# Expert weights of a mixture-of-experts layer loaded in pairs of chunks

## What is computed

```
logits = xf @ w_router + b_router
top_v, top_i = lax.top_k(logits, 4)              # 4 of 32 experts for each token
def expert_block(xblk, e):
    hmid = xblk @ w_up[e] + b_up[e]              # w_up[e]:   1024 x 2048, 8 MB
    hg = minimum(hmid[:, :1024], 7.0)
    hl = clip(hmid[:, 1024:], -7.0, 7.0)
    act = hg * sigmoid(1.702 * hg) * (hl + 1.0)
    return act @ w_down[e] + b_down[e]           # w_down[e]: 1024 x 1024, 4 MB
```

## Time and profile before

| | |
|---|---|
| three timed runs | 1762.39, 1768.26, 1769.11 us; median 1768.26 |
| profiled execution | 1768.84 us, its span 1767.0 us |
| mean granted clock of PE | 0.891 |
| PE busy | 1400.2 us, 79% of the span |
| DVE, ACT, POOL busy | 30%, 13%, 14% |
| HBM read, written | 463.20 MB, 18.74 MB |
| chain that ended last | PE 32%, issue 20%, DMA 10% of the span |
| experts | from 718 us to the end of the loads at about 1720 us |

### The profile page before, as it was taken

The page is one execution under the profiler, slowest core; times in us unless marked ns, Lnnn a source line. Parts: engine busy times, 40 slices in busy tenths (PEclk is TensorE's granted clock), DMA queues, the critical chain, the costliest instruction groups (busy, mean ns, idle before and its releaser), DMA issues.

```text
span 1767.0 us, 30847 instructions
## 1 busy us (share of the span) xinstructions
PE 1400.2 (79%) x11033; PEld 779.5 (44%) x11034; DVE 529.4 (30%) x1242; ACT 229.3 (13%) x556; POOL 247.9 (14%) x352
## 2 busy tenths in 40 slices
PE   5899999978779797666699989668588598766950
PEld 4677777757778454222233433223133133222320
DVE  2899464463441522411111121111111011100114
ACT  2111232222111101000000000000000000000002
POOL 2008301113311520100000000000000000000002
PEclk9999999989985898788899989899789799888975
DMA  7977565351001175499999779999999799999994
GB/s 150 230 147 131 95 109 133 55 151 65 0 1 38 58 220 194 179 416 419 416 420 418 293 298 419 418 418 419 417 419 417 319 410 417 420 417 419 418 378 143
DMA packets 177331, 481.65 MB, mean 273 GB/s; under 512 B 16187, under 2 KB 104891, under 8 KB 144457
## 3 DMA queue, kind: packets, MB, share of 16 engines
q1 hardware_dynamic: 163579, 459.17, 70.7%
q0 software_dynamic: 3920, 15.27, 2.6%
q10 hardware_dynamic: 9792, 6.70, 1.2%
HBM read 463.20 MB, written 18.74 MB: 273 GB/s over the span
## 4 chain that ended last, share of the span: by engine, by line
PE 32%; issue 20%; DMA 10%; DVE 3%; ACT 2%; SPq 2%; POOL 1%; POOLq 0%; DVEq 0%; ACTq 0%
PE bank L950 11%; DMA arena<-in_w_up 10%; PE bank L962 6%; PE bank L918 3%; PE bank L869 2%; PE bank L857 2%; PE bank L936 2%; PE bank L797 2%; PE bank L841 1%; SPq L376 1%; SPq L379 1%; ACT gate L1209 1%; POOL qkv L559 1%; DVE gate L1654 1%; DVE xrow L1699 1%
## 5 line engine op out<-in xcount | busy, mean ns | idle before, releaser
L950 PE MATMUL bank<-arena,gate 128*32 128x512 f32 x3264 | 411.0, 633 | 145.4 <-DMA arena<-in_w_up 145.3
L950 PEld LDWEIGHTS bank<-arena,gate 128*32 128x32 f32 x3264 | 107.7, 113 | 407.2 <-issue 300.1
L636 PE MATMUL bank<-arena 128*128 128x304 f32 x1024 | 269.1, 426 | 5.8 <-DMA arena<-in_w_in 5.1
L1653 DVE TENSOR_SCALAR gate<-bank 128x256 f32<-128x256 f32 x51 | 21.6, 424 | 835.3 <-PE bank L950 835.3
L636 PEld LDWEIGHTS bank<-arena 128*128 128x128 f32 x1024 | 197.9, 194 | 75.8 <-DMA arena<-in_w_in 5.6
L962 PE MATMUL bank<-arena,gate 128*32 128x256 f32 x3264 | 189.6, 384 | 36.3 <-ACT gate L1209 36.3
L559 POOL TENSOR_TENSOR qkv<-qkv 128x192 f32<-128x192 f32 x52 | 32.8, 631 | 940.1 <-DVE qkv L1627 940.1
L962 PEld LDWEIGHTS bank<-arena,gate 128*32 128x32 f32 x3264 | 122.3, 111 | 91.2 <-issue 49.0
L1320 DVE SCALAR_TENSOR_TENSOR acc<-arena,pcol,acc x240 | 126.5, 603 | 0.1
L918 PE MATMUL bank<-qkv 128*32 128x256 f32 (+1 forms) x1248 | 90.2, 406 | 10.4 <-POOL qkv L563 10.4
L936 PE MATMUL bank<-qkv 128*128 128x512 f32 x102 | 60.0, 671 | 39.6 <-DVE gate L1654 28.2
(11 more groups left out here) (308 smaller groups left out, 1327.9 us busy)
## 6 DMA issues: line engine op xcount, KB each, us to landing
arena<-in_w_up SPq DMA_DIRECT2D x256, 1024.0 KB, 12.4
arena<-in_w_down SPq DMA_DIRECT2D x256, 512.0 KB, 8.8
arena<-in_w_in SPq DMA_DIRECT2D x64, 512.0 KB, 9.9
y_d<-gate ACTq DMA_DIRECT2D x204, 32.0 KB, 5.3
y_d<-zs POOLq DMA_DIRECT2D x1, 4608.0 KB, 17.9
arena<-in_w_conf_out SPq DMA_DIRECT2D x8, 512.0 KB, 5.1
arena<-in_state_dn_S SPq DMA_DIRECT2D x8, 512.0 KB, 7.2
arena<-in_w_dn_out SPq DMA_DIRECT2D x1, 4096.0 KB, 17.0
```

The lines of the kernel that those rows point to most:

```text
L636: last = mm(bank[2 * (j % 2) + f][:, 0:T], wring[:, j, k, P * f:P * (f + 1)], rhs[:, k, :], start=(k == 0), stop=(k == KC - 1))
L950: last = mm(hidden(q)[v], xgT[:, i, SL * q0:SL * (q0 + 1)], parts(wup[k], q)[v], start=False, stop=(k == KC - 1), skip_group_check=True)
```

## The change

Two neighbouring chunks are loaded by one transfer. An expert has four transfers of 2 MB for `w_up` and four of 1 MB for `w_down` in place of eight and eight, and the semaphores `up_in` and `down_in` are four each. SP waits once for each pair, until the second chunk of the pair was used (`used + (k + 1)`). PE still goes chunk by chunk and still waits before each, on the pair's semaphore. The buffers, their sizes and places, the order of the loads and all arithmetic stay.

```diff
+        wup2 = [arena[:, 4096 * ((k + 2) % 4):4096 * ((k + 2) % 4 + 1)].rearrange("p (a n) -> p a n", a=2) for k in range(4)]
+        wdn2 = [arena[:, A_PROJ + 2048 * k:A_PROJ + 2048 * (k + 1)].rearrange("p (a n) -> p a n", a=2) for k in range(4)]
...
-        up_in = [sem(f"up_in{i}") for i in range(KC)]
-        down_in = [sem(f"down_in{i}") for i in range(KC)]
+        up_in = [sem(f"up_in{i}") for i in range(KC // 2)]
+        down_in = [sem(f"down_in{i}") for i in range(KC // 2)]
...
             def load_up(e, k):
-                sp.dma_start(wup[k], w_up_v[:, e, k, :]).then_inc(up_in[k], 16)
+                sp.dma_start(wup2[k // 2], w_up_v[:, e, k:k + 2, :]).then_inc(up_in[k // 2], 16)
...
             def load_down(e, k):
-                sp.dma_start(wdn[k], w_dn_v[:, e, k, :]).then_inc(down_in[k], 16)
+                sp.dma_start(wdn2[k // 2], w_dn_v[:, e, k:k + 2, :]).then_inc(down_in[k // 2], 16)
...
-            for k in range(KC):
+            for k in range(0, KC, 2):
                 load_down(0, k)
...
-            for k in range(4):
+            for k in range(0, 4, 2):
                 load_up(0, k)
             sp.wait_ge(s["o_mm_done"], 6)
-            for k in range(4, KC):
+            for k in range(4, KC, 2):
                 load_up(0, k)
...
-                for k in range(KC):
-                    sp.wait_ge(s["up_used"], used + k)
+                for k in range(0, KC, 2):
+                    sp.wait_ge(s["up_used"], used + (k + 1))
                     load_up(e, k)
-                for k in range(KC):
-                    sp.wait_ge(s["down_used"], used + k)
+                for k in range(0, KC, 2):
+                    sp.wait_ge(s["down_used"], used + (k + 1))
                     load_down(e, k)
...
-                    pe.wait_ge(up_in[k], landed)
+                    pe.wait_ge(up_in[k // 2], landed)
...
-                    pe.wait_ge(down_in[k], landed)
+                    pe.wait_ge(down_in[k // 2], landed)
```

## The result

| | before | after |
|---|---|---|
| median of seven runs each | 1768.26 us (1762.39 to 1771.29) | 1777.02 us (1770.54 to 1781.55) |
| profiled execution, its span | 1768.84, 1767.0 us | 1770.54, 1768.8 us |
| ratio after to before | | 1.0055, 95% interval 1.0038 to 1.0073 |

What follows compares the result with a forecast made beforehand. The DMA rate was taken to bound the expert stretches, and PE the pauses between. Release +3.2, landing +1.9 and fewer transfers -3.0 gave +2.1 us, a forecast median of 1770.5 us, range 1760 to 1781 us.

Steps and rivals of the forecast that it cites:

- rival 1: Before each expert's down loads: refill of `w_down` comes too late, up to 14 us more, 1785 us; chance 0.10.
- the forecast's own bounds: All terms taken at their extremes: from +7.9 us to -10.3 us for the whole kernel.
- What bounds the kernel: Expert part: DMA rate sets the end in stretches at 414 to 416 GB/s; PE sets it at the pauses between.
- Fewer transfers: Expert loads: eight of sixteen transfers go, 0.0125 us each, saving 3.0 us in 30 experts.
- Later release: After pauses and at loop start, an expert's first transfer is issued one chunk later: +3.2 us.
- the joints: Loop start and pauses where DMA engines wait for PE; three count, costing 1.08, 1.06 and 1.07 us.
- Later landing: Where PE takes the lead, a chunk waits until both of its pair have landed: +1.9 us.
- (a): In front of the pause at 978 us: chunks 6 and 7 both follow the later landing, 0.9 us more.
- (b): In front of the pause at 1402 us: two chunks instead of one follow the landing of chunk 3, +0.5 us.
- Rivals 2 and 3: Transfers dearer, saving 13 us, 1760 us, chance 0.07; pair moves at another rate, 1% giving 1780 or 1761 us, chance 0.07.
- What the profile would show: Profile after: merged counts, 414 to 418 GB/s, first issue near 731.8 us, three pauses about 1 us longer, 28 `w_up` waits.

Runs made afterwards that it cites:

- the half transfers: Kernel before with every chunk loaded by two transfers of 64 partitions each, 32 transfers an expert for 16; ratio 1.4362, +770 us.
- the fours: Changed kernel taken further: two transfers of 4 MB and two of 2 MB an expert, freed and landed by four chunks; ratio to kernel before 1.0750, +132 us.

## Why the prediction was right or wrong

The forecast was 1770.5 us, within 0.5%, in a range of 1760 to 1781. The measured 1777.02 us is in the range. The ratio lies 0.05 points over the half per cent, and its interval takes in both sides of it. The sum itself was wrong: its +2.1 us are not in the interval of +6.7 to +12.9. That the range holds is the work of the part of rival 1 that it took in and to which 0.10 was given; that is some luck, since the forecast's own bounds ended at +7.9 us. (By its own terms the sum is 1770.4 us, and the bounds of 1776.7 and 1758.5 us are those of the profiled execution, 0.6 us above those for the median.) By its steps:

- **What bounds the kernel** held: the stretches stay at 411 to 416 GB/s, and 6.5 of 7.0 us are in pauses and dips.
- **Fewer transfers, -3.0 us: wrong, it is 0.** The price of 0.0125 us came from 416 against 412 GB/s, a difference of 1% between two stretches of 8 and 10 us. Eight experts in the same stretch of both kernels, 244.39 against 244.38 us, give 0.0002 us for a transfer, and the shortest time of an expert is 30.41 us in both. The lower bound, no saving, was the truth.
- **Later release, +3.2 us: about right.** Alone it cost 4.8 us (2.3 to 7.4). Some of it is not at the joints: 1.8 us are lost at the down issues, a term that the sum did not have. The chunks of a joint can be longer than assumed: in the changed kernel the four chunks at the last pause took 5.65 us for 4.27, with PE's granted clock at 0.52 in that stage for 0.59.
- **Later landing, +1.9 us: mis-sized, it is +8.0.** I counted it only where PE takes the lead, and left waiting tiles out because PE catches up. PE does, but the down loads stand behind it: 4.1 of the 7.6 us of that run's profile are lost at the down issues. The other 4.0 us are in the pauses, for 1.4 us in the sum at the two joints (a) and (b). The run with pair landing ahead of the down projection alone has 6.9 of the 8.0 us; how the rest splits is within the intervals.
- **Rival 1, 0.10: it is what the sum lacked beside the saving.** It costs 3.0 us at the down issues (3.4 in the second profile), as much as the saving that did not come. Its mechanism and its place were right, behind the landing of chunk 3. Its size was not: it would have taken up to 1 us in each of 14 waiting tiles, 1785 us. There are 12 such tiles in both kernels (eight of the 56 waits before stand by themselves, 0.18 to 1.14 us long), and four of the 12 lose over 0.4 us in the changed one. Its margin of 1.7 to 2.7 us was reckoned from PE's wait for chunk 3, which makes 862.36 + 4 x 2.49 - 869.51 = 2.8 us in the expert shown. By the packets 1.5 us of work were left there, and 1.4 and 1.1 us in the other two experts shown, for 2.2 and 2.4 us where there was no dip. So the 1.8 us at which the rival was to decide was near the truth, and the margin that was held against it was over 1 us too long.
- **What the profile would show.** The counts are right. PE waits for `w_up` 162.0 us in 48 pieces, not in 28: two waits in each of 12 tiles, and 24 single ones elsewhere (0.15 to 2.04 us). By the stages the pauses are 11, 9 and 10.5 us for 11, 10 and 9. By lost time they are 1.5, 0.1 and 1.8 us longer, and 1.6, 1.7 and 2.3 us in the second profile of the changed kernel, so "about 1 us each" was somewhat too little. The first issue came at 726.23 us and not near 731.8, since the mixer was over earlier. The sign for rival 1, a dip before the down loads, is there, but in some experts and not in each; how often it comes in a timed run is not known.

Rivals 2 and 3 fall: neither a saving of 13 us nor another rate was there.

## What to carry to other kernels

Where transfers stood in a queue, merging them saved nothing here, while each merge moved a release and a landing by one chunk. Count the cost of a later landing through everything that stands behind it, up to the next issue: here landing, chunk, gather, down projection, and then SP's down loads with all later loads behind them. Reckon the margin in bytes that are still to move, not from the moment at which PE hears of a landing. In these kernels 3 us of work in the queue at an issue were enough and less than 2 us were not. A little time gained on PE in that chain can be worth more than elsewhere: 0.66 us a tile brought some 2 us in one kernel and some 10 in the other.

## What the runs showed of the hardware

- A transfer's own cost in a full queue is not measurable: 64 of 512 KB and 1 MB fewer changed 244.39 us by 0.01 us.
- What a queue needs to stay full, over the 372 first down issues in twelve profiles (all but those of the half transfers and of the fours): with 3 us of work or more left by the packets (197 issues) at most 0.2 us were lost, with 2 to 3 us (129) 0.1 us in the mean and up to 0.9, with less than 2 us (46) 0.7 us in the mean and up to 2.1.
- The first packet came 0.96 to 0.99 us after the issue in the four places of the kernel before where the queue was empty.
- One landing is counted by 16 increments of its semaphore, and they are spread: for the last up chunks before the dip at 870 us from 870.33 to 872.26 us, for an issue at 869.51; in the kernel before from 782.96 to 784.75 us, for an issue at 780.74. So an estimate of the last landing tells too late when the first DMA engine has nothing to do. That the engines which end first cause the dip fits this; it was not shown by itself.
- Transfers of 512 and 256 KB into 64 partitions ran at 226 GB/s, those of 1 MB and 512 KB into 128 at 415.
